# Latent projections squared one product later, their norms taken behind a gate product, and short products woven between value blocks

## The reference

```python
def second_block(x, ...):
    h = rmsnorm_2(x, norm_g)
    (q_lat, c_kv, k_rope, z_a, q_b, k_b, v_b, z_b,
     q_idx, k_idx, w_idx, gate_a, gate_b) = jnp.split(h @ w_in, cuts, axis=-1)
    q = rmsnorm_2(q_lat, g_q_lat) @ w_uq               # 384 -> 8 heads x 96
    kv = rmsnorm_2(c_kv, g_kv_lat) @ w_ukv             # 256 -> keys and values of 8 heads
    q_pe, k_pe = rope(...), rope(k_rope)
    y_a = mla_attention(q_nope, q_pe, k_nope, k_pe, v_a, pos) * jax.nn.silu(z_a)
    # score = sum over 8 index heads of relu(q_idx k_idx) * w_idx; the best 128 keys of each query
    y_b = dsa_attention(q_b, k_b, v_b, q_idx, k_idx, w_idx, rel_bias, pos, topk) * jax.nn.silu(z_b)
    merged = (jax.nn.sigmoid(gate_a) * (y_a @ w_o_a) + jax.nn.sigmoid(gate_b) * (y_b @ w_o_b))
    return rmsnorm_2(x + merged @ w_out, final_g)
```

## Time and profile before

| | |
|---|---|
| time, median of 3 runs | 1094.46 us (1094.31 to 1095.98) |
| the profiled execution | 1095.55 us |
| its span, first to last instruction | 1093.8 us |
| PE (TensorE matmul) busy | 1052.5 us, 96% of the span |
| DVE busy | 609.8 us, 56% |
| ACT busy | 460.0 us, 42% |
| POOL busy | 252.1 us, 23% |
| mean granted TensorE clock | 0.986 |

### The profile page before, as it was taken

The page is one execution under the profiler, slowest core; times in us unless marked ns, Lnnn a source line. Parts: engine busy times, 40 slices in busy tenths (PEclk is TensorE's granted clock), DMA queues, the critical chain, the costliest instruction groups (busy, mean ns, idle before and its releaser), DMA issues.

```text
span 1093.8 us, 13481 instructions
## 1 busy us (share of the span) xinstructions
PE 1052.5 (96%) x5152; PEld 846.5 (77%) x5160; DVE 609.8 (56%) x1049; ACT 460.0 (42%) x808; POOL 252.1 (23%) x155
## 2 busy tenths in 40 slices
PE   7989999999999999999999998899999999999996
PEld 6867787777888888888888776677787767788885
DVE  6584366656544432444445466898756666425544
ACT  6425445545222311222234465545754544423322
POOL 1362332222010100001014333322323223321100
PEclk9998899999999999999999999899999999999998
DMA  7211143212222232232332326212222333222312
GB/s 280 74 59 60 39 118 98 75 45 95 96 97 98 95 116 96 77 102 91 108 105 77 128 61 213 78 42 75 64 82 82 98 109 106 74 86 91 108 66 77
DMA packets 34799, 102.32 MB, mean 94 GB/s; under 512 B 4560, under 2 KB 8032, under 8 KB 34736
## 3 DMA queue, kind: packets, MB, share of 16 engines
q1 hardware_dynamic: 34736, 101.47, 28.3%
HBM read 93.35 MB, written 4.74 MB: 90 GB/s over the span
## 4 chain that ended last, share of the span: by engine, by line
PE 75%; DVE 12%; ACT 5%; issue 4%; SPq 2%; DMA 1%; POOL 1%; DVEq 0%; ACTq 0%; POOLq 0%
PE bank L1379 20%; PE bank L1383 20%; PE bank L1381 20%; PE bank L1513 3%; PE bank L1504 2%; PE bank L1393 2%; PE bank L1394 2%; PE bank L1395 2%; DVE m L2079 1%; DVE score L2070 1%; DVE score L2081 1%; PE bank L1485 1%; DVE acc L1835 1%; DVE g_S L1934 1%; ACT WH L1565 1%
## 5 line engine op out<-in xcount | busy, mean ns | idle before, releaser
L1379 PE MATMUL bank<-HH,WH 128*128 128x512 f32 x808 | 328.4, 406 | 7.1 <-ACT HH L1573 6.0
L1383 PE MATMUL bank<-HH,WL 128*128 128x512 f32 x808 | 317.3, 393 | 0.0
L1381 PE MATMUL bank<-HL,WH 128*128 128x512 f32 x808 | 317.2, 393 | 0.0
L2162 POOL TENSOR_TENSOR WL<-WS,WH 128x1024 fp32r<-128x1024 f32 x64 | 155.0, 2421 | 358.0 <-ACT WH L1565 357.4
L1379 PEld LDWEIGHTS bank<-HH,WH 128*128 128x128 f32 x808 | 153.8, 190 | 42.4 <-issue 10.5
L1565 ACT ACTIVATE WH<-WS 128x1024 fp32r<-128x1024 f32 x161 | 167.5, 1047 | 41.9 <-PE bank L1383 41.0
L1383 PEld LDWEIGHTS bank<-HH,WL 128*128 128x128 f32 x808 | 152.9, 189 | 33.2
L1381 PEld LDWEIGHTS bank<-HL,WH 128*128 128x128 f32 x808 | 153.3, 190 | 29.3 <-issue 0.5
L1816 DVE TENSOR_TENSOR WL<-WS,WH 128x1024 fp32r<-128x1024 f32 x97 | 126.4, 1310 | 34.1 <-ACT WH L1565 34.1
L2210 POOL TENSOR_TENSOR fa<-fa,fg 128x512 f32<-128x512 f32 x22 | 28.3, 1285 | 273.4 <-DVE fa L2016 273.4
L1379 PE MATMUL bank<-GH,WH 128*128 128x512 f32 x176 | 68.5, 389 | 0.0
(11 more groups left out here) (335 smaller groups left out, 1731.9 us busy)
## 6 DMA issues: line engine op xcount, KB each, us to landing
WS<-wall SPq DMA_DIRECT2D x161, 512.0 KB, 3.4
scratch<-rows SPq DMA_DIRECT2D x8, 320.0 KB, 5.4
X<-xT SPq DMA_DIRECT2D x8, 256.0 KB, 6.9
b_t<-scratch SPq DMA_DIRECT2D x8, 256.0 KB, 3.6
outT<-X SPq DMA_DIRECT2D x8, 256.0 KB, 2.1
b_m<-b_m SPq DMA_DIRECT2D x11, 128.0 KB, 2.3
f_s<-f_s SPq DMA_DIRECT2D x8, 128.0 KB
f_m<-f_m SPq DMA_DIRECT2D x8, 128.0 KB
```

Of the source, the lines that this page charges most:

```text
L1379: e.matmul(b[:, :], wh, xh[:, at_k, :], start=k == 0, stop=False)
L1381: e.matmul(b[:, :], wh, xl[:, at_k, :], start=False, stop=False)
L1383: m = e.matmul(b[:, :], wl, xh[:, at_k, :], start=False, stop=k == n - 1)
L2162: e.tensor_tensor(WL[:, u % NW, :], WS[:, u % NST, :], f32(WH[:, u % NW, :]), ALU.subtract).then_inc(*tick(w_low_g, u))
```

## The change

It has six parts.

- In `latents`, the square and the two halves of a latent (`rest`) are no longer issued right behind its `latent` step, but behind the first pair of the next product.
- The sums and Ln of `lk` move from behind `ql0` to behind the second pair of `za0`. The sums of `lq` and `norm_q` move from the third pair of `za0` to behind its tanh, and all three Exp stand in `norm_q`. The product `za1` moves from `mla_products(1)` to right behind this.
- The index scores start after 7 yields of the side work where they started after 9, and `now["per"]` is 0.7 where it was 0.6, so a few more top-k rounds fall beside them.
- The four blocks of `mla_v` stand between `uk0`, `uq0` and `uq1` instead of ahead of them. `unit_end` is told that their weights are held until the last block.
- The 7 DMAs that spread the keys are issued in a step `send_keys` of their own, behind `norm_q`.
- The gate product `ga1` moves from the `dsa` attention to the `mla` attention, and the rate in the `dsa` attention is 0.82 where it was 0.85.

No computation is added or taken away.

```diff
@@ -923,7 +923,7 @@
         do("keys", t1=t1, free1=free1, t2=t2, free2=free2)
         tmp_ring.give(m1, rope("end"))
         tmp_ring.give(m2, rope("end"))
-        now["per"] = 0.6
+        now["per"] = 0.7
 
         def index_scores():
             for i in (3, 2, 1):
@@ -949,35 +949,48 @@
             def out(b):
                 m, t, free = tmp_ring.take()
                 do("latent", c=c, x=x, name=name, b=b, t=t, free=free)
-                add_square((x, c), total_g, t[:, :], None, out_v(name))
-                do("halve_latent", c=c, x=x, t=t, name=name)
-                tmp_ring.give(m, low((x, c)))
-                known.add((x, c))
+
+                def rest():
+                    add_square((x, c), total_g, t[:, :], None, out_v(name))
+                    do("halve_latent", c=c, x=x, t=t, name=name)
+                    tmp_ring.give(m, low((x, c)))
+                    known.add((x, c))
+                squares.append(rest)
                 return out_v(name)
             return out
 
+        squares = []
+
+        def with_squares(gen):
+
+            for n, _ in enumerate(gen):
+                if n == 0 and squares:
+                    squares.pop(0)()
+                yield n
+
         def latents():
             for c in range(2):
-                yield from product(f"ckv{c}", "w_in_2", 0, cols(P_CKV + 128 * c), "h3", NK,
-                                   lat_out(c, "lk", f"ckv{c}", acc[1]))
+                yield from with_squares(product(f"ckv{c}", "w_in_2", 0, cols(P_CKV + 128 * c), "h3", NK,
+                                                lat_out(c, "lk", f"ckv{c}", acc[1])))
             bias_rows()
             do("row_out")
             for c in range(3):
-                yield from product(f"ql{c}", "w_in_2", 0, cols(P_QL + 128 * c), "h3", NK,
-                                   lat_out(c, "lq", f"ql{c}", acc[0]))
+                yield from with_squares(product(f"ql{c}", "w_in_2", 0, cols(P_QL + 128 * c), "h3", NK,
+                                                lat_out(c, "lq", f"ql{c}", acc[0])))
                 do("copy_rows", heads=((0, 1, 2), (3, 4, 5), (6, 7))[c])
-                if c == 0:
+            for n in with_squares(z_products("za", P_ZA, 0)):
+                if n == 1:
                     i1, b1 = column_sums("lk", acc[1], total_g(("lk", 1)))
                     i2, b2 = token_sums("lkt", [acc[1]], total_g(("lk", 1)))
                     do("norm_kv", b1=b1, b2=b2)
-                    t_ring.give(i1, norm_a("lk ln"))
                     t_ring.give(i2, norm_a("lkt ln"))
-            for n, _ in enumerate(z_products("za", P_ZA, 0)):
-                if n == 2:
-                    i, b = column_sums("lq", acc[0], total_g(("lq", 2)))
-                    do("norm_q", b=b)
-                    t_ring.give(i, norm_a("lq ln"))
                 yield
+            t_ring.give(i1, norm_a("lk ln"))
+            i, b = column_sums("lq", acc[0], total_g(("lq", 2)))
+            do("norm_q", b=b)
+            t_ring.give(i, norm_a("lq ln"))
+            do("send_keys")
+            yield from z_products("za", P_ZA, 1)
 
         def mla_v():
             even()
@@ -986,7 +999,7 @@
                 column = sum((cols(hd * 128 + 64, 64) for hd in range(4 * c2, 4 * c2 + 4)), ())
                 for k in range(2):
                     tiles.append((tile(("w_ukv_2", k, column[:128])), c2, k))
-                    tile(("w_ukv_2", k, column[128:]))
+                    unit_end[tile(("w_ukv_2", k, column[128:])) // UT] = ("av", 3)
             for tb in range(4):
                 i, b, free = d_ring.take()
                 do("mm_av", tb=tb, tiles=tiles, b=b, free=free)
@@ -1025,12 +1038,18 @@
                     known.add(f"uq{hd}")
                     return out_v(f"uq{hd}")
                 return out
+            between = mla_v() if p == 0 else iter(())
+            if p == 0:
+                yield next(between)
             yield from product(f"uk{p}", "w_ukv_2", 0, cols(256 * p, 64) + cols(256 * p + 128, 64), "lk", 2, k_out)
             for hl in range(2):
                 hd = 2 * p + hl
+                if p == 0:
+                    yield next(between)
                 yield from product(f"uq{hd}", "w_uq_2", 0, cols(96 * hd, 96) + cols(96 * hd + 80, 16)
                                    + cols(96 * hd + 64, 16), "lq", 3, q_out(hd, hl))
-            if p:
+            yield from between
+            if p > 1:
                 yield from z_products("za", P_ZA, p)
             mla_in[p] = slots
 
@@ -1045,8 +1064,8 @@
                     "to": "ya", "to_n": p, "z": z, "z_ring": z_ring, "z_i": z_i}
 
         now["low"] = w_low_g
-        side = chain(latents(), mla_v(), mla_products(0))
-        for _ in range(9):
+        side = chain(latents(), mla_products(0))
+        for _ in range(7):
             next(side)
         i, b, free = t_ring.take()
         do("index_weights", b=b, free=free)
@@ -1154,8 +1173,9 @@
         def mla_side():
             yield from mla_products(1)
             yield from dsa_products(0)
+            yield from gate_a(0)
             yield from mla_products(2)
-            yield from gate_a(0)
+            yield from gate_a(1)
             yield from mla_products(3)
             yield from dsa_v()
             dsa_bias(0)
@@ -1165,7 +1185,6 @@
             yield from z_products("zb", P_ZB, 1)
             yield from dsa_products(2)
             yield from z_products("zb", P_ZB, 2)
-            yield from gate_a(1)
             yield from dsa_products(3)
             yield from gated_ya(1)
             yield from z_products("zb", P_ZB, 3)
@@ -1186,7 +1205,7 @@
         weave(attention([(lambda p=p: p in mla_in and f"za{p}" in gates, lambda p=p: mla_pair(p)) for p in range(4)]
                         + [(lambda p=p: dsa_ready(p), lambda p=p: dsa_pair(p))
                            for p in range(4)],
-                        pc_ring, pt_ring), side, [0.9] * 66 + [0.85])
+                        pc_ring, pt_ring), side, [0.9] * 66 + [0.82])
 
         assert not behind and not first
 
@@ -1327,7 +1346,7 @@
                         r, dst = slice(32 * h, 32 * h + 32), i_qq[4 * j + h]
                         q.wait_ge(istack_v(("q", j)))
                         e.dma_start(f32(dst[32:64, 128:T]), f32(i_ql[r, j, 128:T])).then_inc(*index_in[j].tick())
-                elif kind == "keys":
+                elif kind == "send_keys":
                     for n in range(1, 8):
                         r = slice(64, 96) if n < 4 else slice(96, 128)
                         q.wait_ge(rope("end"))
@@ -1773,14 +1792,14 @@
                     q.wait_ge(sums("lkt"), norm_v("n3t log"))
                     e.activation(rtok[:, 4:8], s["b2"][:, 0:4], ACT.Ln, scale=1.0 / 256, bias=eps[:, :]).then_inc(
                         *norm_a.tick("lkt ln"))
-                    q.wait_ge(norm_a("lk ln"))
-                    e.activation(RK[:, :], RK[:, :], ACT.Exp, scale=-0.5).then_inc(*norm_a.tick("lk"))
-                    q.wait_ge(norm_a("lkt ln"))
-                    e.activation(rtok[:, 4:8], rtok[:, 4:8], ACT.Exp, scale=-0.5).then_inc(*norm_a.tick("lkt"))
                 elif kind == "norm_q":
                     q.wait_ge(sums("lq"))
                     e.activation(RQ[:, :], s["b"][:, :], ACT.Ln, scale=1.0 / 384, bias=eps[:, :]).then_inc(
                         *norm_a.tick("lq ln"))
+                    q.wait_ge(norm_a("lkt ln"))
+                    e.activation(rtok[:, 4:8], rtok[:, 4:8], ACT.Exp, scale=-0.5).then_inc(*norm_a.tick("lkt"))
+                    q.wait_ge(norm_a("lk ln"))
+                    e.activation(RK[:, :], RK[:, :], ACT.Exp, scale=-0.5).then_inc(*norm_a.tick("lk"))
                     q.wait_ge(norm_a("lq ln"))
                     e.activation(RQ[:, :], RQ[:, :], ACT.Exp, scale=-0.5).then_inc(*norm_a.tick("lq"))
                 elif kind == "merge_gate":
```

## The result

The changed kernel took **1098.93 us** (median of 6 runs, 1098.14 to 1099.27), the kernel before 1094.38 us in the same comparison (6 runs): a ratio of 1.0043, with an interval of 1.0032 to 1.0054. The change costs 4.6 us. The profiled execution of after took 1099.27 us and its span is 1097.5 us, 3.7 longer than that of before.

A forecast was written before the change was run, and what follows sets the result against it. PE, busy 96% of the span, was taken as the bound, with at most 13.7 us to win. Terms 1.5 + 0 - 0.5 + 1.5 = +2.5 us on the median 1094.46 gave 1097.0 us, range 1091.0 to 1101.0.

The forecast's parts named there:

- Its signs: Profile: `uk0` waits 4 to 8 us for `zb`, DVE idles 3 to 5 before `RQ`, half speed at 700, `Pc` wait near 880.
- its three terms: Behind `uq2`: clock 0, `mla` attention -0.5 us and `dsa` attention +1.5 us.
- First section: To the sum of squares: first index score waits 0.9 us; `ql2`'s latent ends at 679.1, later less 0.7 for collisions.
- The top-k rounds at 678.25 and 679.04: On DVE before the change: they kept their 0.69 and 0.68 us, read as not blocked by POOL.
- the lower bound: Earliest end of `ql2`'s latent, with as little blocking as before: 672.4, also when PE delivers `ql2`.
- Second section: From the latent of `ql2` to `uq2`: `uk0` waits 6.8 us; `uq2` at 714.5, 2.2 us behind, taken as 1.5.
- Clock: Half-speed stretches behind the 6.8 and 2.2 us waits: first nearly free, second 1.7 us as before, so 0.
- The `mla` attention: `ga1` replaces `za1`, four top-k rounds fewer; PE's 0.9 us wait may go: -0.5 us (0 to -0.9).
- The `dsa` attention: Loses `ga1` (5.4 us of cover) and 3% of the rest: +1.5 us, bounds 0 and 4.
- DVE isn't late: Rival: POOL's work falls mostly into top-k rounds and latents, DVE up to 7 us earlier: 1089.1 to 1092.2; faster, chance 0.19.
- The long fall of the clock: Rival: 10 us at half speed after the 6.8 us wait, `dsa` waits at their upper end: +7.2, 1101.6; chance 0.07.

The follow-up runs named there:

- experiment 7: Changed kernel with the low halves of the units beside the index scores made by DVE instead of POOL: 1094.76 us, ratio 1.0004 to before.
- 9: Kernel before with the low halves beside the index scores made by DVE instead of POOL: 1091.84 us, ratio 0.9969 to before.
- experiment 5: Changed kernel with `za1` back behind the second pair's queries, and `ga1` and the `dsa` rate as before: 1095.61 us, ratio 1.001.
- 11: Changed kernel with the `lq` sum and `norm_q` ahead of `za0`'s tanh, and `za1`, `ga1` and the rate back: 1092.91 us, ratio 0.9981.
- 12: Changed kernel with `lq` sum and `norm_q` ahead of `za0`'s tanh, `za1`, `ga1` and rate back, low halves on DVE: 1089.87 us, ratio 0.9949.
- kernel 1: Changed kernel with `ga1` put back into the `dsa` attention and the rate there back at 0.85: 1097.71 us, ratio 1.003.
- experiment 2: Kernel before with only `ga1` moved into the `mla` attention and the `dsa` rate at 0.82: 1096.8 us, ratio 1.0025.
- 4: Changed kernel with only `za1` put back behind the queries of the second pair of heads: 1095.66 us, ratio 1.0011.
- experiment 3: Changed kernel with `norm_q` (Ln, Exp and DVE's `RQ`) issued behind `za1` and its tanh: 1101.48 us, ratio 1.0065.
- experiment 6: Changed kernel with the sum of `lq` and `norm_q` ahead of the tanh of `za0`: 1095.39 us, ratio 1.0004.

## Why the prediction was right, and where its terms were off

I predicted slower, 1097.0 us, and it is slower, 1098.93. The mechanism is the one that the prediction's sum walks through: a chain over ACT and DVE from the latent of `ql2` to the bank of `za1`. Its signs came too: the longest wait is at `uk0` for `zb`, DVE idles 3.87 us before `RQ`, a stretch at half the clock begins at 698.3 and PE waits for `Pc` at 884; only the sum of `lq` waits for `rtok` and not for `RK`, both of the same `norm_kv`. But that the sum behind `uq2` is off by only 0.8 us is luck: its three terms are off by 1.7, 1.4 and 1.1, and cancel in part. The terms one by one (ends of instructions where the prediction gives ends):

- **First section.** The index score waits 0.80 us (0.9). The latent of `ql2` ends at 679.62 (679.1). I then took off 0.7 because not every collision need happen; they all did: each of POOL's seven operations from 655 to 677 us met a score or the low half of a latent on DVE. The cause, POOL's low halves, is shown by experiments 7 and 9. Two readings in the prediction don't hold. The top-k rounds at 678.25 and 679.04 don't show that POOL leaves them alone, since POOL idled from 677.4 to 681.65; the rounds that did run beside POOL, in this kernel and all others, do show it (the last section). And the lower bound adds up to 672.0, not 672.4.
- **Second section.** The sum waits 2.86 us (3.1), the gate is scaled at 686.96 (686.8), DVE idles 3.87 us before `RQ` (4), `za1` is scaled at 700.07 (700.2), PE waits 6.28 us (6.8) and `uq2` starts at 714.36 (714.5). The lag there is 714.36 - 712.3 = 2.1 us, where I took 1.5. The waits inside it came out otherwise. Those of 2.1 us for a relu and 0.7 at the second value block aren't there, and `uq0` waited 0.32 us and not 2.2. In their place stand the two stretches at half the clock, which the walk had left out here: from the first index score to `uq2` it has 15.8 us of waits, and the trace has 10.3 of waits and 4.2 lost at half the clock.
- **Clock, predicted 0.** This step failed in its parts. I expected one fall behind the wait at `uk0` and one behind that at `uq0`. The first is there, 6.8 us long, and mostly hidden before `uq0`, as I had said of it; one of 3.4 us behind the sum's wait ends before PE waits for `za1`. The fall that I charged behind `uq0` doesn't come; the wait that was to begin it is 0.32 us. Counted from `uq2` on, before has one (1.7 us lost) and after none: -1.7.
- **The `mla` attention, predicted -0.5.** The mis-sized term with the wrong sign: its waits went from 1.1 to 2.0 us, +0.9. I had let the old 0.9 us wait for `Pc` go; 0.68 of it stayed, and one of 1.10 us for `acc`, the merging of a gate, came. Whose the latter is stays open: kernels 5, 11 and 12 show it (1.4 us) with `ga1` in its old place and kernel 1 doesn't, and kernels 2 and 4, with `ga1` in its new one, don't show it either.
- **The `dsa` attention, predicted +1.5.** Mis-sized too: from 1.6 to 4.2 us, +2.6. Two waits became 1.57 and 1.46 us; experiment 2 shows the same edit at +1.5 us of waits and 2.3 us of time.
- **Together** from `uq2` to the last `mix`: -1.7 + 0.9 + 2.6 = +1.8, and the trace shows 949.09 - 945.18 less the 2.1 there already, 1.8. I had +1.0. So the lag is 3.9 us in place of 2.5. The remaining 0.7 of the 4.6 us lies in which executions were profiled: that of before took 1.2 us more than its median, that of after 0.3, and behind the last `mix` after is 0.2 us shorter.

Of the rivals, "DVE isn't late" had nothing to stand on, since POOL's operations met scores and low halves, not top-k rounds. The long fall of the clock didn't come in the changed kernel, but in two of the experiments: 10.2 us in experiment 7, from inside a wait of 5.2, and 13.6 in experiment 3, where two waits follow each other.

**What stays open.** The same move of `ga1` costs 2.3 us in the kernel before, 1.2 in the changed one and nothing in experiment 5's; In the changed kernel and experiment 5's the move took waits from the `mla` attention and put them into the `dsa` attention; in the kernel before both grew (1.1 to 1.7 and 1.6 to 3.1 us). What decides it I can't show. The waits and the clock account for too much in experiments 3, 4 and 6. Half of the busy time is a little too much for what the clock costs: in the changed kernel a 128x512 matmul follows the one before after 0.43 us at half the clock and 0.23 at full, so some 46% is lost; for experiment 3 that takes off only 0.4 us. And the value blocks between the products and the earlier scores were never measured by themselves.

## What to carry to other kernels

Before a product is put where it may cover a wait, follow who must give its bank back: `za1` covered nothing, because its own bank came free behind the chain that it was to hide, and cost 3.3 us. A step on ACT has all its consumers to be counted, and functions should stand in an order that shares their table loads (Ln, Ln, Exp, tanh: two loads less, and 3.5 us here with `norm_q` no longer behind the gate). And when operations on DVE take two to five times what they take alone, look at what GpSimd does beside them before moving anything: handing the low halves to DVE gained the most of the single edits (4.2 us, against 3.5 and 3.3), and with the norms first and `za1` and `ga1` back it beats the kernel before by 5.0 us.

## What the runs showed of the hardware

- A stretch at half the clock can begin inside a wait and then costs less than half its length: the one of 6.8 us in the changed kernel holds 4.97 us of work, 2.5 us lost. The lengths recorded between 640 and 1000 us are 3.4, 6.8, 10.2 (experiment 7) and 13.6 us; the longest begins 1.5 us behind a wait of 1.9 us and holds one of 4.8.
- A score that starts on DVE while POOL makes a low half ends only behind it: those of 128x256 elements took 0.48 us alone and up to 2.47, ending 0.3 us behind POOL's operation. The steps of a top-k round (0.68 to 0.70 and 0.68 us) and the latents read from a bank (0.68 to 0.69) took the same beside POOL as alone, in every kernel in which they met it. One input from SBUF doesn't make an operation safe: the first head's score, a TENSOR_SCALAR over one such tile, took 0.35 us in the changed kernel, and in the kernel before, beside a low half on POOL from 674.70 to 677.39, 2.37:

```profile
675.24 2.37 DVE L2067 TENSOR_SCALAR score<-i_t,wi 128x384 f32<-128x384 f32 x1
```

- The tanh behind an Exp has no table load, while each Ln behind a tanh, and each Exp behind a Ln, has one of 1.28 us (experiment 6 and the changed kernel).
